# Row maxima of both score blocks of an attention unit in one VectorE instruction, with both exponentials behind it, in a two-layer diffusion backbone

## The chip, the cores and the metric

The kernel runs on one core of a Trainium2 chip, as one program. The metric is the time of that core on the device in microseconds (us); lower is better. TensorE (PE) multiplies matrices, VectorE (DVE) and ScalarE (ACT) work elementwise, GpSimd (POOL) gathers, and each engine runs its own instructions in the order in which they are written. Engines wait for each other through semaphores alone: an instruction behind a wait that is not yet met stays where it is, and so does all that is queued behind it on the same engine.

## What is computed

Two layers, each of them a normalisation, a combined projection, three token mixers side by side (RWKV-7 time mixing, differential attention, a gated linear recurrence), an output projection, and then a retrieval of experts with product keys. The change lies in the differential attention. For each head and each block of 128 queries there are two score blocks, `c = 0` and `c = 1`, of half the head's dimension each:

```python
s = jnp.einsum('bhqcd,bhkcd->bhcqk', qi, k).astype(jnp.float32) * scale
p = jax.nn.softmax(s, axis=-1)
p = p[:, :, 0] - lam * p[:, :, 1]
return jnp.einsum('bhqk,bhkd->bhqd', p.astype(v.dtype), v)
```

The softmax takes the maximum of each row off before the exponential, so each block needs its row maxima first. The 512 latent tokens attend to 768 keys (512 of their own and 256 cached), the 128 prompt tokens to 128.

## The kernel before

One stage per layer, `mix_stage`, runs the RWKV-7 scan and the attention together. Nothing is planned at run time: the order is written out by hand as a list of **slots**, and every engine walks the same list. The scan is the backbone of it. It has 5 steps of 14 hops (`HOPS`: pairs, lower, square1 to square5, inverse, rhs0, sa0, state0, rhs1, sa1, state1), so 70 slots. In each slot PE does the products of the hop (`hop`), DVE and sometimes ACT take them out of PSUM (`take`), and PE starts the next hop when DVE has raised `byv` and, after the square hops, ACT has raised `bya`.

The attention is laid into those slots as 40 **units** per layer (`UNITS`: one head, one block of 128 tokens; units 0 to 31 are latent with 768 keys, units 32 to 39 are prompt with 128). Slots are counted in threes. In the first slot of three, the even unit 2p gets its scores, row maxima and exponentials; in the third, the odd unit 2p+1. In between stands the second slot, where earlier units get their products with the values. For one unit the chain is:

- `scores` on PE (L1245, or L1248 to L1252): both blocks into PSUM banks 4 to 7. The banks are not doubled, so it first waits for `e_done`, until both exponentials of the unit before are through.
- `row_max` on DVE (L1444): one reduction for each block, each raising `m_ready`.
- `exps` on ACT (L1323): one exponential for each block with the negated maximum as bias and the row sum as accumulated output (a separate read of the accumulator follows each); each raises `e_done`.
- `weights` on DVE (L1449, L1450): reciprocals of the sums, after both exponentials. Then `scale_second` on ACT (L1328), `combine` on DVE (L1458), `turn` on PE (L1265, transposes through PSUM bank 3), `take_turned` on ACT (L1335), `values` on PE (L1284) and `out` on DVE (L1464), which also frees bank 3 (`o_taken`) for the next `turn`.

The order on each engine within a slot matters here. PE: the hop, `turn` of the first half of an older unit, `scores` of the new unit, `turn` of the second half. DVE: the hop's `take`, then in first slots `combine` and `weights` of the unit before, then `row_max` of the new unit; in second slots `weights` of the even unit, `combine`, `out`. ACT: the hop's `take` (copies L1339, L1346, L1349, L1354), `take_turned`, in first slots `scale_second` of the odd unit before, and at the end `exps` of the new unit. So the exponentials stand directly ahead of ACT's copy for the next hop. PE also multiplies some filler (L1133) in hops where it would idle.

Of the kernel before, what the change touches and what calls it, by code (L numbers as in the profile page):

```python
# [31 lines left out]
ALU = mybir.AluOpType  # L32
ACT = mybir.ActivationFunctionType
AX = mybir.AxisListType

P = 128
# [960 lines left out]
KH = 3 * P  # L997


def key_halves(u):  # L1000

    return 2 if UNITS[u][1] < TILES - 1 else 1


def half_count(u, half):

    return sum(key_halves(i) for i in range(u)) + half + 1


def is_unit(u):  # L1010
    return 0 <= u < len(UNITS)


def both_halves(u):
    return range(key_halves(u)) if is_unit(u) else ()
# [5 lines left out]
def mix_stage(g, l, keep):  # L1021
# [17 lines left out]
    s_ready, m_ready, e_done, r_ready, scaled = (  # L1039
        g.sem(x) for x in ("scores_ready", "row_max_ready", "exps_ready", "weights_ready", "second_scaled"))  # L1040
    comb, t_ready = g.sem("probs_combined"), g.sem("probs_transposed")
    pt_ready, o_ready, o_taken = g.sem("probsT_ready"), g.sem("attn_out_ready"), g.sem("attn_out_taken")
    A, B, C, W, S = 0, 1, 2, 3, 4
    OUT = CA * P
    with ExitStack() as st, nc.Block() as block:
# [13 lines left out]
        p = g.sb(st, "p", [P, 2, 2, 2, KH])  # L1059
        pd = g.sb(st, "pd", [P, 2, 2 * KH])  # L1060
        pt = g.sb(st, "pt", [P, 2, 2 * KH])
        mx = g.sb(st, "mx", [P, 2, 2])
# [13 lines left out]
        def scores_of(u, c):  # L1076

            b = S + 2 * c
            return g.ps[:, b:b + 2, 0:KH] if key_halves(u) == 2 else g.ps[:, b:b + 1, 0:P]

        def probs_of(u, c):
            return p[:, u % 2, c, :, :] if key_halves(u) == 2 else p[:, u % 2, c, 0:1, 0:P]

        def flat_probs(u, c):
            whole = p[:, u % 2, c, :, :].rearrange("p k n -> p (k n)")
            return whole if key_halves(u) == 2 else whole[:, 0:P]

        def half_keys(u, k):

            return slice(k * KH, (k + 1) * KH) if key_halves(u) == 2 else slice(0, P)  # L1090

        @block.sync
        def _(sync):
            sync.dma_start(mask[:, :, :], d["consts"][:, CI["maskF"][0]:CI["maskF"][0] + 4 * CH]).then_inc(loaded, 16)
            sync.dma_start(low[:, :, :], d["consts"][:, CI["lowF"][0]:CI["lowF"][0] + 3 * CH]).then_inc(loaded, 16)
            sync.wait_ge(zeroed, 1)
            for h in range(2):
                rows = slice(h * HD, (h + 1) * HD)
                sync.dma_start(sz[rows, :, :, h * HD:(h + 1) * HD], d["state_rwkv"][l, h]).then_inc(state_in, 16)

            sync.wait_ge(final, 1)
            for h in range(2):
                rows = slice(h * HD, (h + 1) * HD)
                sync.dma_start(d["new_rwkv"][l, h], sz[rows, :, :, h * HD:(h + 1) * HD]).then_inc(stored, 16)
# [212 lines left out]
        @block.scalar  # L1317
        def _(act):
            def exps(u, c):
                act.wait_ge(m_ready, 2 * u + c + 1)  # L1320
                if u >= 2:
                    act.wait_ge(comb, u - 1)
                nc.scalar.activation(probs_of(u, c), scores_of(u, c), ACT.Exp,  # L1323
                                     bias=mx[:, u % 2, c:c + 1], accum_out=sm[:, u % 2, c:c + 1]).then_inc(e_done, 1)

            def scale_second(u):
                act.wait_ge(r_ready, u + 1)
                nc.scalar.activation(flat_probs(u, 1), flat_probs(u, 1), ACT.Copy, scale=sm[:, u % 2, 3:4]).then_inc(scaled, 1)  # L1328

            def take_turned(u, k):  # L1330
                keys = half_keys(u, k)
                act.wait_ge(t_ready, half_count(u, k))
                if u >= 2:
                    act.wait_ge(o_ready, u // 2)
                nc.scalar.activation(pt[:, u % 2, keys], g.ps[:, W, 0:keys.stop - keys.start], ACT.Copy).then_inc(pt_ready, 1)  # L1335

            def take_keys(n):
                act.wait_ge(bt_ready, n)
                nc.scalar.activation(bt[:, (n - 1) % 2, :, :].rearrange("p i n -> p (i n)"), g.ps[:, (B, C)[n % 2], :], ACT.Copy).then_inc(bt_taken, 1)  # L1339

            def take(slot, step, name):
                if name.startswith("square"):
                    act.wait_ge(ready, slot + 1)
                    n = int(name[6:])
                    if n == 1:
                        nc.scalar.activation(pw, by_unit(A), ACT.Copy).then_inc(bya, 1)  # L1346
                        take_keys(2 * step + 2)
                    else:
                        nc.scalar.activation(pwt[:, (n + 1) % 2, :, :], by_unit(C), ACT.Copy).then_inc(bya, 1)  # L1349
                elif name == "lower":  # L1350
                    take_keys(2 * step + 1)
                elif name == "inverse":
                    act.wait_ge(tok_ready, step + 1)
                    nc.scalar.activation(tv[:, :, :], g.ps[:, B, :].rearrange("p (i n) -> p i n", i=2), ACT.Copy).then_inc(tok_taken, 1)  # L1354

            for slot, (step, name) in enumerate(SLOTS):
                take(slot, step, name)
                pair, third = divmod(slot, 3)
                if third == 1:
                    if is_unit(2 * pair):  # L1360
                        scale_second(2 * pair)
                else:
                    u, fresh = (2 * pair - 3, 2 * pair) if third == 0 else (2 * pair - 2, 2 * pair + 1)
                    for k in both_halves(u):
                        take_turned(u, k)
                    if third == 0 and is_unit(fresh - 1):
                        scale_second(fresh - 1)
                    if is_unit(fresh):
                        for c in range(2):
                            exps(fresh, c)  # L1370

        @block.vector
        def _(ve):
# [65 lines left out]
                                    o.did(last)  # L1439
                return last  # L1440

            def row_max(u, c):
                ve.wait_ge(s_ready, u + 1)
                ve.tensor_reduce(mx[:, u % 2, c:c + 1], scores_of(u, c), AX.XY, ALU.max, negate=True).then_inc(m_ready, 1)  # L1444

            def weights(u):

                ve.wait_ge(e_done, 2 * u + 2)
                o.then(ve.reciprocal(sm[:, u % 2, 2:4], sm[:, u % 2, 0:2]))  # L1449
                ve.tensor_scalar(sm[:, u % 2, 3:4], sm[:, u % 2, 3:4], g.lam[:, 1:2], None, ALU.mult).then_inc(r_ready, 1)  # L1450

            def combine(u):

                ve.wait_ge(scaled, u + 1)
                if u >= 2:
                    ve.wait_ge(t_ready, half_count(u - 2, key_halves(u - 2) - 1))
                n = flat_probs(u, 0)
                ve.scalar_tensor_tensor(pd[:, u % 2, 0:n.shape[-1]], n, sm[:, u % 2, 2:3], flat_probs(u, 1),  # L1458
                                        ALU.mult, ALU.add).then_inc(comb, 1)

            def out(u):
                h, t = UNITS[u]
                ve.wait_ge(o_ready, u // 2 + 1)
                ve.tensor_copy(g.outT[:, CA + h // 2, t * P:(t + 1) * P], g.ps[:, W, KH:KH + P]).then_inc(o_taken, 1)  # L1464
# [5 lines left out]
            for slot, (step, name) in enumerate(SLOTS):  # L1470
                ve.wait_ge(ready, slot + 1)
                nx += name in XSUMS
                take(step, name, nx).then_inc(xsum if name in XWITH else byv, 1)
                if step == TILES - 1 and name == "state1":
                    ve.wait_ge(byv, slot + 1)
                    ve.sem_inc(final, 1)
                pair, third = divmod(slot, 3)
                if third == 0:
                    if is_unit(2 * pair - 2):
                        combine(2 * pair - 2)  # L1480
                    if is_unit(2 * pair - 1):
                        weights(2 * pair - 1)
                elif third == 1:
                    if is_unit(2 * pair):
                        weights(2 * pair)
                    if is_unit(2 * pair - 1):
                        combine(2 * pair - 1)
                    if is_unit(2 * pair - 3):
                        out(2 * pair - 3)
                if third != 1 and is_unit(2 * pair + third // 2):  # L1490
                    for c in range(2):
                        row_max(2 * pair + third // 2, c)
    return stored


# [1494 lines left out]
```

## Time and profile before

| | |
|---|---|
| median of 3 runs | 4174.37 us (4172.11 to 4175.89) |
| profiled execution, first to last instruction (its span) | 4170.2 us |
| what the median has over the span | 4.2 us |
| PE busy | 3967.5 us, 95% |
| DVE busy | 3319.0 us, 80% |
| ACT busy | 1514.5 us, 36% |

The profile gives no other time of the profiled execution than its span; 4.2 us is what the median of the runs lies above it. Busy time says how long an engine had an instruction in work, not that it set the pace. Times in rows are microseconds from the start of the span, unless marked ns. `x2` at the end of a row of the timeline says that two instructions of the same kind stand in it one after the other. An idle time in brackets names the instruction that ended it.

### The profile page before, as it was taken

To read this page: it belongs to the slowest core of one execution; us is meant where nothing else is said; L and a number is where in the kernel's file an instruction comes from. 1 tells how busy PE (TensorE), PEld (TensorE's weight loads), DVE (VectorE), ACT (ScalarE), POOL (GpSimd) and SP (SyncE) were. 2 spreads that over 40 slices of the span, in tenths; PEclk is the share of its full clock that TensorE was granted. 3 is DMA by queue.
4 is the path that set the end of the run, shared out by engine and by line. 5 is a ranking of instruction groups with operands and counts; after the bars stand their busy time and mean duration, and the time that the engine had idled before them with its cause. 6 is when DMAs were issued, how large, how long until landed. Compare 5 with 4: busy or idle time off the path is not lost. (4 is left out here: it accounts for less than half of the span.)

```text
span 4170.2 us, 69350 instructions
## 1 busy us (share of the span) xinstructions
PE 3967.5 (95%) x25830; PEld 3126.4 (75%) x25830; DVE 3319.0 (80%) x6259; ACT 1514.5 (36%) x2457; POOL 1426.5 (34%) x1046
## 2 busy tenths in 40 slices
PE   7999988999999999999989999889999999999997
PEld 5977767655567888888879677775555788888886
DVE  3556753799998999999955676538999899999997
ACT  3435643211164333333353355321112633333333
POOL 0010000265414656666500000004644066566662
PEclk8999999999999999999999899899999999999998
DMA  6230013799999999999822300157998999999996
GB/s 254 71 137 6 2 38 117 246 369 333 342 302 356 393 400 398 406 404 404 346 92 60 127 2 2 53 179 294 350 342 320 302 391 407 389 408 403 404 406 252
DMA packets 410253, 1095.17 MB, mean 263 GB/s; under 512 B 38288, under 2 KB 181008, under 8 KB 403344
## 3 DMA queue, kind: packets, MB, share of 16 engines
q1 hardware_dynamic: 262544, 554.96, 36.9%
q0 software_dynamic: 147456, 536.94, 33.2%
q8 instruction: 147, 2.41, 0.2%
q14 instruction: 106, 0.87, 0.1%
HBM read 1013.90 MB, written 77.86 MB: 262 GB/s over the span
## 5 line engine op out<-in xcount | busy, mean ns | idle before, releaser
L1822 POOL DMA_INDIRECT ring<-peer_u_rows,rows x512 | 670.5, 1310 | 1785.0 <-DVEq L2176 1077.6
L1822 POOL DMA_INDIRECT ring<-peer_v,rows x512 | 731.4, 1428 | 431.3 <-DVE acc L2663 359.2
L1779 PE MATMUL ps<-h,u 128*128 128x384 f32 x2112 | 700.3, 489 | 3.4 <-PEq L1895 2.5
L2663 DVE SCALAR_TENSOR_TENSOR acc<-ring,act,acc 128x1024 f32<-128x1024 f32 x508 | 643.1, 1279 | 1.7
L1826 DVE SCALAR_TENSOR_TENSOR ring<-ring,acc 128x1024 f32<-128x1024 f32 x512 | 613.7, 1219 | 34.4 <-PEq L2292 22.7
L200 PE MATMUL ps<-vhi,wlo 128*128 128x512 f32 x1536 | 603.9, 393 | 22.0 <-DVE wlo L2642 21.0
L201 PE MATMUL ps<-vlo,whi 128*128 128x512 f32 x1536 | 600.7, 391 | 0.0
L202 PE MATMUL ps<-vhi,whi 128*128 128x512 f32 x1536 | 600.5, 391 | 0.0
L1779 PEld LDWEIGHTS ps<-h,u 128*128 128x128 f32 x2112 | 396.1, 191 | 261.9 <-issue 6.8
L2627 DVE TENSOR_TENSOR vlo<-v,vhi 128x1024 fp32r<-128x1024 f32 x256 | 312.4, 1220 | 77.9 <-ACT vhi L2570 71.4
L200 PEld LDWEIGHTS ps<-vhi,wlo 128*128 128x128 f32 x1536 | 289.6, 189 | 91.2 <-issue 32.4
L200 PE MATMUL ps<-xhi,ulo 128*128 128x384 f32 x992 | 332.6, 335 | 2.6 <-DVE ulo L2623 2.6
L202 PEld LDWEIGHTS ps<-vhi,whi 128*128 128x128 f32 x1536 | 289.4, 188 | 60.7
L201 PEld LDWEIGHTS ps<-vlo,whi 128*128 128x128 f32 x1536 | 289.6, 189 | 58.7
L202 PE MATMUL ps<-xhi,uhi 128*128 128x384 f32 x992 | 332.7, 335 | 0.0
L201 PE MATMUL ps<-xlo,uhi 128*128 128x384 f32 x992 | 332.2, 335 | 0.0
L2570 ACT ACTIVATE vhi<-v 128x1024 fp32r<-128x1024 f32 x256 | 269.1, 1053 | 117.4 <-DMA v<-peer_v 105.1
L1950 PE MATMUL ps<-h,query_raw 128*128 128x128 f32 (+1 forms) x1024 | 295.3, 443 | 8.5 <-ACT h L419 8.4
L1790 ACT ACTIVATE hh<-ps 128x384 f32<-128x384 f32 x256 | 123.1, 481 | 440.6 <-PE ps L1779 396.3
L2575 ACT ACTIVATE whi<-u 128x384 fp32r<-128x384 f32 x128 | 63.7, 525 | 599.8 <-DVE u L2637 599.8
L1950 PEld LDWEIGHTS ps<-h,query_raw 128*128 128x128 f32 x1024 | 162.7, 197 | 126.1 <-issue 115.0
L200 PE MATMUL ps<-hhi,proj_lo 128*128 128x320 f32 x672 | 211.7, 315 | 24.3 <-DVE hlo L439 24.3
(356 smaller groups left out, 7092.2 us busy)
## 6 DMA issues: line engine op xcount, KB each, us to landing
u<-peer_u SPq DMA_DIRECT2D x256, 512.0 KB
v<-peer_v SPq DMA_DIRECT2D x256, 512.0 KB
gates<-stage SPq DMA_DIRECT2D x24, 1984.0 KB, 9.7
sel<-gates SPq DMA_DIRECT2D x62, 768.0 KB
query_raw<-peer_wq SPq DMA_DIRECT2D x64, 512.0 KB
hidden<-hh SPq DMA_DIRECT2D x128, 192.0 KB
u<-hidden SPq DMA_DIRECT2D x128, 192.0 KB
mod_ring<-mod_late SPq DMA_DIRECT2D x20, 1024.0 KB, 8.5
```

Source lines behind the costliest of these rows:

```text
L200: pe.matmul(out, lhs[1], rhs[0], start=start, stop=False)
L201: pe.matmul(out, lhs[0], rhs[1], start=False, stop=False)
L202: return pe.matmul(out, lhs[0], rhs[0], start=False, stop=stop)
L1779: mm = pe.matmul(self.g.ps[:, bank, 0:ND], self.u[:, slot, kc, :], self.x[:, kc, 0:ND], start=(kc == 0), stop=(kc == KC - 1))
L1790: return self.g.nc.scalar.activation(self.hh[:, slot, :], self.g.ps[:, slot, 0:ND], ACT.Gelu)
L1822: return pool.indirect_dma_start(to, None, table, rows)
L1826: return ve.scalar_tensor_tensor(row, row, 1.0, self.acc[:, x, :], ALU.mult, ALU.mult, accum_out=self.act[x][:, slot:slot + 1])
L1950: return pe.matmul(g.ps[:, SUMS + i % 2, 0:width(i)], raw[:, i % Q_RING, kc, :], h[:, kc, tokens_of(i)], start=(kc == 0), stop=(kc == KC - 1))
L2570: nc.scalar.activation(v2[0][:, j, :], v[:, j % 2, :], ACT.Copy).then_inc(v_hi, 1)
L2575: nc.scalar.activation(w2[0][:, j, :], h, ACT.Copy).then_inc(w_hi, 1)
L2627: ve.tensor_tensor(v2[1][:, j, :], v[:, j % 2, :], v2[0][:, j, :].bitcast(F32), ALU.subtract).then_inc(v_lo, 1)
L2663: ve.scalar_tensor_tensor(acc, r, w, acc, ALU.mult, ALU.add).then_inc(used, 1)
```

## The change

The two reductions of a unit become one, over both blocks, which writes both maxima and raises `m_ready` once. Both exponentials wait for that one.

```diff
@@ mix_stage, ACT
             def exps(u, c):
-                act.wait_ge(m_ready, 2 * u + c + 1)
+                act.wait_ge(m_ready, u + 1)
@@ mix_stage, DVE
-            def row_max(u, c):
+            def row_max(u):
                 ve.wait_ge(s_ready, u + 1)
-                ve.tensor_reduce(mx[:, u % 2, c:c + 1], scores_of(u, c), AX.XY, ALU.max, negate=True).then_inc(m_ready, 1)
+                both = g.ps[:, S:S + 4, :].rearrange("p (c k) n -> p c k n", c=2)
+                scores = both[:, :, :, 0:KH] if key_halves(u) == 2 else both[:, :, 0:1, 0:P]
+                ve.tensor_reduce(mx[:, u % 2, :], scores, AX.XY, ALU.max, negate=True).then_inc(m_ready, 1)
@@ the slot loop, DVE
                 if third != 1 and is_unit(2 * pair + third // 2):
-                    for c in range(2):
-                        row_max(2 * pair + third // 2, c)
+                    row_max(2 * pair + third // 2)
```

## Rows read from the trace of the kernel before

**Rows 1.** The page: the span.

```profile
span 4170.2 us, 69350 instructions
```

**Rows 2.** Busy time of each engine in the two mixing stretches, one per layer.

```profile
core 0: us, PE busy (x) PEld busy (x) DVE busy (x) ACT busy (x) POOL busy (x), PEclk, DMA share, GB/s
320.00:590.00 270.00, 250.26 (x3981) 197.90 (x3974) 179.17 (x369) 147.48 (x308) 0.00 (x0) 0.96 0.01 3
2370.00:2640.00 270.00, 250.49 (x3942) 198.12 (x3942) 178.07 (x367) 147.47 (x308) 0.00 (x0) 0.95 0.01 2
```

**Rows 3.** Waits in 320 to 590: us in total, times, longest us.

```profile
PEld ps L1248 <- ACT p L1323: 7.0, 8, 1.2
```

**Rows 4.** Groups by line and shape on DVE: count, busy us, mean ns, idle before.

```profile
L1444 DVE TENSOR_REDUCE mx<-ps 128x1 f32<-128x768 f32 x128 | 116.4, 951 | 49.4 <-PE ps L1252 49.4
L1444 DVE TENSOR_REDUCE mx<-ps 128x1 f32<-128x128 f32 x32 | 7.7, 283 | 4.4 <-PE ps L1245 4.4
L2168 DVE TENSOR_REDUCE sm<-res 128x8 f32<-128x128 f32 x10 | 2.8, 280 | 0.0
```

**Rows 5.** Timeline around unit 5: start us, us, engine, line, idle time in brackets.

```profile
360.64 1.82 DVE L1444 TENSOR_REDUCE mx<-ps 128x1 f32<-128x768 f32 x2 [1.89 <-PE ps L1252]
...
361.63 0.90 ACT L1323 ACTIVATE p<-ps,mx 128x768 f32<-128x768 f32 x1
...
363.31 0.20 ACT L1323 ACTIVATION_READ_ACCUMULATOR p<-ps,mx 128x1 f32 x1
...
363.56 0.30 PEld L1248 LDWEIGHTS ps<-proj 32*128 32x128 f32 x4 [1.16 <-ACT p L1323]
```

**Rows 6.** Timeline behind units 3 and 11: last sum, next scores.

```profile
351.08 0.20 ACT L1323 ACTIVATION_READ_ACCUMULATOR p<-ps,mx 128x1 f32 x1
...
351.69 0.30 PEld L1248 LDWEIGHTS ps<-proj 32*128 32x128 f32 x4 [0.17 <-issue]
...
404.88 0.20 ACT L1323 ACTIVATION_READ_ACCUMULATOR p<-ps,mx 128x1 f32 x1
...
405.88 0.30 PEld L1248 LDWEIGHTS ps<-proj 32*128 32x128 f32 x4 [0.17 <-issue]
```

**Rows 7.** Timeline: PE's hop behind unit 2.

```profile
343.46 1.04 PEld L1165 LDWEIGHTS ps<-pwt,px 64*64 64x64 f32 x32 [1.73 <-DVE px L1407]
```

**Rows 8.** Timeline around unit 14, up to PE's wait for the combined weights.

```profile
421.23 1.82 DVE L1444 TENSOR_REDUCE mx<-ps 128x1 f32<-128x768 f32 x2 [0.87 <-PE ps L1252]
...
422.91 0.89 ACT L1323 ACTIVATE p<-ps,mx 128x768 f32<-128x768 f32 x1
...
424.80 0.17 DVE L1449 RECIPROCAL sm<-sm 128x2 f32<-128x2 f32 x1 [1.43 <-ACT p L1323]
...
426.46 0.31 PEld L1265 LDWEIGHTS ps<-keep,pd 128*128 128x128 f32 x3 [1.28 <-DVE pd L1458]
```

**Rows 9.** Timeline around unit 16, the same chain.

```profile
434.92 1.81 DVE L1444 TENSOR_REDUCE mx<-ps 128x1 f32<-128x768 f32 x2
...
436.02 0.89 ACT L1323 ACTIVATE p<-ps,mx 128x768 f32<-128x768 f32 x1
...
439.57 0.31 PEld L1265 LDWEIGHTS ps<-keep,pd 128*128 128x128 f32 x3 [1.29 <-DVE pd L1458]
```

**Rows 10.** Timeline behind unit 22: ACT's copy for the hop, and the hop.

```profile
479.18 0.60 ACT L1349 ACTIVATE pwt<-ps 128x512 f32<-128x512 f32 x1
...
480.02 1.01 PEld L1188 LDWEIGHTS ps<-px,pwt 64*64 64x64 f32 x32 [0.17 <-issue]
```

**Rows 11.** Timeline: maxima of units 24 and 25, first and second layer.

```profile
488.67 1.82 DVE L1444 TENSOR_REDUCE mx<-ps 128x1 f32<-128x768 f32 x2 [1.13 <-PE ps L1252]
497.35 1.82 DVE L1444 TENSOR_REDUCE mx<-ps 128x1 f32<-128x768 f32 x2 [0.59 <-PE ps L1252]
...
2536.91 1.82 DVE L1444 TENSOR_REDUCE mx<-ps 128x1 f32<-128x768 f32 x2 [1.13 <-PE ps L1252]
2547.17 1.82 DVE L1444 TENSOR_REDUCE mx<-ps 128x1 f32<-128x768 f32 x2 [0.59 <-PE ps L1252]
```

**Rows 12.** Clock in a stretch between the last two (columns as in Rows 2).

```profile
2537.80:2541.00 3.20, 3.20 (x26) 2.43 (x24) 1.74 (x6) 2.72 (x7) 0.00 (x0) 0.50 0.00 0
```

**Rows 13.** Timeline: PE's longest wait in the first stretch.

```profile
566.46 0.86 PEld L1143 LDWEIGHTS ps<-ar,proj 64*64 64x64 f32 x32 [2.75 <-DVE outT L1437]
```

## The prediction

> **What bounds the kernel now.** I read the page first: PE is busy for 95% of a span of 4170.2 us [rows 1], so at first sight nothing on DVE matters. But the changed instructions lie in two stretches only, one per layer, so I read the busy times there: in each 270 us PE is busy for 250, DVE for 179, ACT for 147 [rows 2]. No engine is full. PE has some 20 us of idle time per stretch, and the work goes round in a circle: PE makes products, DVE and ACT take them, PE waits for the taking. The question is thus which waits of PE end on the chain that the change lengthens. The waits in the stretch answer it: PE's load of query weights for the next unit's scores waits 8 times for an exponential, 7.0 us in all [rows 3], and the second layer's stretch shows the same wait with the same count and sum.
>
> The timeline of one of them, unit 5, shows the chain [rows 5]. The two reductions start at 360.64 and end together 1.82 us later. The first exponential starts at 361.63, 0.99 us after the first reduction started: that is its 0.95 us [rows 4] and 0.04 of signal. Both exponentials and the reads of their sums end at 363.51, and 0.05 us later PE starts the next scores. PE had then idled for 1.16 us. The second reduction lies wholly beside the first exponential. So the chain is: first maximum, two exponentials, PE. That is what the change touches.
>
> **The merged instruction.** It replaces two of 951 ns (768 elements) by one over 1536, in 32 units per layer, and two of 283 ns (128 elements) by one over 256 in 8 units. From the two shapes an element costs (951 - 283) / 640 = 1.04 ns [rows 4]. So 951 + 768 x 1.04 = 1.75 us, and 0.42 us for the short ones. A second result in each partition should cost nothing: the reduction with eight results takes 280 ns where one result takes 283 [rows 4]. Bounds: 1.60 us if the fixed part shrinks to nothing, and 1.90 us, twice the single one. I take 1.75, since two in a row take 1.82 with two fixed parts [rows 5]. DVE is freed by 0.07 us per unit. The first exponential, though, no longer starts at R + 0.99 (R: start of the reduction) but at R + 1.75 + 0.04 = R + 1.79. Everything behind it comes 0.80 us later, unless ACT was held until later anyway. That is the price, and the places where it counts follow.
>
> **Odd units (third slots).** ACT's only other work ahead of the exponentials is the copy of turned weights, which ends at about R + 0.96, so the full 0.80 us is lost. What PE feels is 0.80 less its slack beyond the 0.05 us of signal. I went through all units of the first layer for the distance from the last sum to PE's next scores. Units 1, 5, 7, 9, 13, 23, 25 and 27 have 0.05 us (unit 5 in [rows 5]), so these cost 8 x 0.80 = 6.40 us. Units 3, 19 and 31 have 0.41 (unit 3: 351.28 to 351.69 [rows 6]), 0.43 each, 1.29 us. Units 11, 17, 21 and 29 have 0.80 (unit 11: 405.08 to 405.88 [rows 6]), 0.03 to 0.05 each, 0.18 us. Unit 15 has more and costs nothing. The prompt units cost almost nothing, since their reductions lie under ACT's other work; 0.08 us at unit 35. Behind unit 31 a short unit follows, and ACT's next two copies then hold PE's second turn: 0.28 us more.
>
> **Even units (first slots).** Here ACT first rescales the odd unit before. In units 6, 8, 14, 20, 24, 26 and 28 that holds the exponential until R + 1.68 (unit 14: 421.23 to 422.91 [rows 8]), so only 0.11 us is lost. In units 0, 2, 4, 10, 12, 16, 18, 22 and 30 DVE itself was late, R is late, and 0.38 to 0.81 us are lost at the exponential. PE does not wait for these exponentials directly, but for two chains behind them:
>
> - Sums, weights, combination, `out`, then PE's turn. At unit 14 DVE idles 1.43 us for the sum and PE 1.28 us for DVE [rows 8]: 0.11 us. At unit 16 the exponential starts at R + 1.10 [rows 9], and 1.79 - 1.10 = 0.69 us arrive at PE's wait at 439.57. At unit 18, 0.40, and at unit 4, 0.12 on top of what unit 3 has already shifted.
> - ACT's copy for the next hop, queued behind the exponentials. At unit 22 it ends at 479.78 and PE starts at 480.02 [rows 10]; a loss of 0.66 less 0.24 of slack, with 0.05 to 0.10 of signal, is 0.47 us beyond unit 21. At unit 30, 0.45; at unit 12, 0.09; at unit 28, 0.09; at unit 0, 0.36.
>
> Unit 2 adds nothing: PE's hop at 343.46 [rows 7] waits for this copy and for DVE, and both were going to come 0.80 us later, DVE because PE is shifted behind unit 1, ACT because of unit 2. The two delays lie side by side. Unit 10 is covered in the same way by unit 9.
>
> The even terms come to 0.11 + 0.69 + 0.40 + 0.12 + 0.47 + 0.45 + 0.09 + 0.09 + 0.36 = 2.78 us. With the odd terms, 6.40 + 1.29 + 0.18 + 0.08 + 0.28 = 8.23 us, it is 11.0 us per layer and **22.0 us** for both.
>
> Does a later wait swallow it? PE's delay arises before it does the new scores, so all that DVE and ACT do from those is delayed too, and the next waits shift with it. The one exception is a wait for something DVE began before PE was delayed; I found that at unit 17 alone, worth 0.03 us. What DVE gains, 0.07 us, ends in DVE's own waits for PE (49.4 us idle ahead of the maxima alone [rows 4]).
>
> **The clock.** PE's waits grow from 1.16 to nearly 2 us at five odd units per layer, and unit 16's likewise. In the second layer such a wait, of the same size as unit 5's, was followed by a stretch at a granted clock of 0.50, the 1.2 GHz level [rows 12]. Between the maxima of units 24 and 25 passed 10.26 us there, and 8.68 in the first layer, which kept its clock [rows 11]: 1.58 us lost. Of some 20 waits of 1.0 to 1.8 us in both layers one had that; of the two of 2.75 us (the first in [rows 13]) both had. Waits of 2 us lie in between, a dozen of them. I take three more such stretches, 4.7 us; bounds none and ten, 0 to 16 us. The Trainium skill ("TensorE: Matmul & The Clock Gate", What's actually happening) says that the throttled state is the default and activity releases it; the two rows agree as far as they go.
>
> **The sum**, against the profiled execution: 4170.2 + 22.0 + 4.7 = 4196.9 of span, and with the 4.2 us that the median has over the span, 4201.1 us, +0.64%. The bounds of the merged instruction, 1.60 and 1.90 us, move the 17 or so terms of a layer by 0.15 each: 5 us less or more. The likeliest case's own range is 4190 to 4212.
>
> **The rivals.**
> - *Delays that lie side by side* (0.14). As at unit 2, more of the terms may overlap than I saw: PE waits for both an engine that it delayed itself and one that was late by itself. If it is half of all terms, 11 us remain, 4185; if two thirds, 7 us, 4181.5, which counts as no change. For it: the even units where DVE was late. Against: the largest terms are waits with nothing else due.
> - *The clock falls often* (0.09): ten stretches or more, 22 + 16 and up, 4212 to 4225. For it: rows 11 and 12; against: one in twenty now.
> - *DVE is relieved and that decides* (0.03), the faster side. In a third of the slots DVE's maxima run straight into the next take. Should PE wait for DVE behind them nearly everywhere, the saving of 0.07 us counts for each of 80 units, 5 us, 4169. It decides only where ACT is held beyond R + 1.79 for other reasons, which no latent unit shows. The Trainium skill ("VectorE: DVE Perf Modes", Rules for kernel authors) speaks for this change: it says to minimise the number of operations, since each one drains the pipe. By that rule the pair costs twice 0.95 us and the merge saves 0.15 us a unit, 12 us in all, 4162. The trace shows 1.82 for the pair, so less than half of that.
> - *The reduction does not run as one* or runs at another rate (0.02): at 1.90 us and beyond, 4206 and up. The same page (The perf-mode tier table) gives this operation one rate only; rows 4 agree with 1.04 ns per element. A rate that would bring 1536 elements under 0.95 us, from where the exponentials would come no later, is thus not to be expected.
>
> **How the numbers follow.** The main case has 0.72. What a measurement of this kernel can tell from no change is about 0.2%, 8 us. Slower by more than that: the main case, the clock, the slow reduction, and about half of the side-by-side case, together 0.90. Within 8 us: the rest of the side-by-side case and half of the relieved one, 0.08. Faster: 0.02. The range goes from 4184, which takes in the half-overlapping case, to 4215, which takes in ten clock stretches' lower part.
>
> **What would show it.** The reduction at 1.75 us, 64 long and 16 short ones in place of 160; the first exponential of odd units at R + 1.79; PE's wait for the exponential in 11 or more places per layer instead of 9 and of about 2 us where it was 1.16; the stretch from the first to the last maximum 11 us longer per layer; nothing changed between the stretches. I am wrong if the reduction takes far from 1.75 us, if PE's waits grow but the stretch does not, or if the stretches with a granted clock of 0.50 multiply.

## The result, and the profile after

The changed kernel takes 4221.3 us in the median of 4 runs (4215.8 to 4236.1), the kernel before 4175.1 us (4172.1 to 4177.8): a ratio of 1.0119, with an interval of 1.0100 to 1.0138. A second series on another occasion gave 1.0123 (1.0100 to 1.0146). It is slower by some 50 us. The forecast was slower too, but by 27 us, with a range that ended at 4215. The time lies outside of it.

The profiled execution of the changed kernel is the longest of its four, 4236.1 us with a span of 4234.2, so it is 64 us above the span of rows 1. The page first:

```profile
span 4234.2 us, 69270 instructions
PE 4013.8 (95%) x25830; PEld 3157.9 (75%) x25830; DVE 3318.0 (78%) x6179; ACT 1514.6 (36%) x2457; POOL 1425.0 (34%) x1046
```

80 instructions fewer, all of them on DVE (6179 for 6259). PE does the same 25830 products, yet is busy for 46 us more. The products are as many, so they got slower, and the clock is the first thing to ask. The groups by line and shape on DVE answer to rows 4:

```profile
L1446 DVE TENSOR_REDUCE mx<-ps 128x2 f32<-128x1536 f32 x64 | 112.3, 1755 | 62.9 <-PE ps L1252 62.8
L1446 DVE TENSOR_REDUCE mx<-ps 128x2 f32<-128x256 f32 x16 | 6.7, 420 | 4.4 <-PE ps L1245 4.1
```

1755 and 420 ns: the merged instruction runs as it was estimated, 1.75 and 0.42 us. The timeline around unit 5 answers to rows 5 (start, duration, engine, line; idle time in brackets):

```profile
366.76 1.76 DVE L1446 TENSOR_REDUCE mx<-ps 128x2 f32<-128x1536 f32 x1 [1.89 <-PE ps L1252]
...
368.56 0.90 ACT L1323 ACTIVATE p<-ps,mx 128x768 f32<-128x768 f32 x1 [0.83 <-DVE mx L1446]
...
370.23 0.20 ACT L1323 ACTIVATION_READ_ACCUMULATOR p<-ps,mx 128x1 f32 x1
...
370.48 0.30 PEld L1248 LDWEIGHTS ps<-proj 32*128 32x128 f32 x4 [1.96 <-ACT p L1323]
```

The first exponential starts 1.80 us after the reduction where it was 0.99, and PE's wait is 1.96 us instead of 1.16. ACT is now idle for 0.83 us ahead of the exponential. Unit 22 answers to rows 10: ahead of PE's next hop, where PE had been idle for 0.17 us, it is now idle for 0.61 us. The profile names no releaser here ("issue"), but ACT's copy had ended 0.07 us before the hop started, where it had been 0.24 us.

```profile
502.25 1.75 DVE L1446 TENSOR_REDUCE mx<-ps 128x2 f32<-128x1536 f32 x1
...
505.80 0.59 ACT L1349 ACTIVATE pwt<-ps 128x512 f32<-128x512 f32 x1
...
506.46 1.04 PEld L1188 LDWEIGHTS ps<-px,pwt 64*64 64x64 f32 x32 [0.61 <-issue]
```

The waits of the first mixing stretch answer to rows 3 (total, times, longest): 13 where there were 8, and 2.0 us at most.

```profile
PEld ps L1248 <- ACT p L1323: 15.2, 13, 2.0
```

Now the two stretches from the first to the last maximum of a layer, as busy times of each engine with the granted clock in the column behind POOL. First the kernel before:

```profile
324.60:583.50 258.90, 239.85 (x3829) 189.84 (x3831) 174.19 (x358) 145.03 (x300) 0.00 (x0) 0.96 0.01 2
2373.00:2634.80 261.80, 242.90 (x3831) 192.20 (x3833) 174.32 (x358) 145.01 (x300) 0.00 (x0) 0.95 0.01 2
```

and the changed one:

```profile
329.00:619.20 290.20, 263.99 (x3825) 207.73 (x3827) 173.50 (x319) 145.29 (x300) 0.00 (x0) 0.88 0.01 2
2411.40:2697.50 286.10, 259.86 (x3823) 204.56 (x3825) 173.29 (x318) 145.57 (x300) 0.00 (x0) 0.89 0.01 2
```

Of the 64 us, 55.6 lie here (576.3 for 520.7). The other 8.4 us are not shown to come from the change: a second profile of the changed kernel, further below, is 55.5 us above rows 1, and 55.3 of them lie in the same two stretches. DVE and ACT are as busy as before; PE is busy for 41 us more. The clock has only two levels here, 1.00 and 0.50, so a mean of 0.88 over 290.2 us is 2 x 0.12 x 290.2 = 70 us at the lower one. The printed mean is rounded to 0.01, which over such a stretch can hide some 2.6 us. So the times at the lower clock from here on are summed from windows laid around each fall: 43 us for both stretches before and 133 us after, a rise of 90 us. These are the five falls of the kernel before:

```profile
324.60:332.70 8.10, 7.02 (x118) 6.17 (x119) 4.41 (x10) 3.69 (x7) 0.00 (x0) 0.50 0.01 2
568.20:578.40 10.20, 8.85 (x128) 7.48 (x128) 5.54 (x17) 3.25 (x13) 0.00 (x0) 0.50 0.01 2
2373.00:2380.70 7.70, 6.62 (x116) 5.78 (x116) 4.12 (x9) 3.40 (x6) 0.00 (x0) 0.50 0.00 0
2537.70:2541.10 3.40, 3.40 (x30) 2.63 (x26) 1.94 (x6) 2.92 (x7) 0.00 (x0) 0.50 0.00 0
2616.20:2629.80 13.60, 12.31 (x170) 10.39 (x170) 6.76 (x22) 3.93 (x14) 0.00 (x0) 0.50 0.01 1
```

Two of them are the tail of a lower clock that the stretch begins with, two stand at the wait of 2.75 us near its end, and only 3.4 us lie anywhere between. The changed kernel has sixteen. Within its first stretch it looks like this:

```profile
358.00:371.60 13.60, 11.46 (x162) 8.50 (x160) 8.78 (x15) 8.35 (x17) 0.00 (x0) 1.00 0.01 2
371.80:381.80 10.00, 10.00 (x89) 8.23 (x87) 4.80 (x9) 4.01 (x7) 0.00 (x0) 0.50 0.01 2
460.50:477.40 16.90, 16.90 (x147) 13.03 (x145) 9.16 (x18) 5.94 (x12) 0.00 (x0) 0.50 0.00 1
```

The clock falls some 1.2 us after unit 5's wait of 1.96 us has ended, and stays down for 10 us. After unit 16's wait it stays down for 17 us: the maxima of units 17 and 18 are 9.85 us apart where they were 7.28 (441.67 to 448.95). Beside the lower clock that this stretch begins with, it falls seven times in it, each time within 1.5 us of the end of a wait of 1.49 to 1.98 us: at units 5, 7, 9, 16, 23, 25 and 27. DVE's rows of the changed kernel:

```profile
372.34 1.76 DVE L1446 TENSOR_REDUCE mx<-ps 128x2 f32<-128x1536 f32 x1 [1.46 <-PE ps L1252]
385.02 1.76 DVE L1446 TENSOR_REDUCE mx<-ps 128x2 f32<-128x1536 f32 x1 [2.03 <-PE ps L1252]
...
462.32 1.76 DVE L1446 TENSOR_REDUCE mx<-ps 128x2 f32<-128x1536 f32 x1 [2.73 <-PE ps L1252]
472.17 1.75 DVE L1446 TENSOR_REDUCE mx<-ps 128x2 f32<-128x1536 f32 x1
```

The first two are units 6 and 7: 12.68 us, and 8.86 before.

### The profile page after: what moved, and what is told of

Read it like the earlier page. It is cut to its first block and busy times, and to the rows that moved or that the text cites. A ratio compares the mean times of both kernels' runs of the same rounds, so it can differ in the third digit from the quotient of the medians.

```text
span 4234.2 us, 69270 instructions
## 1 busy us (share of the span) xinstructions
PE 4013.8 (95%) x25830; PEld 3157.9 (75%) x25830; DVE 3318.0 (78%) x6179; ACT 1514.6 (36%) x2457; POOL 1425.0 (34%) x1046
```

## The experiments

Theory A has two parts. The first exponential starts later, which costs latency, 22 us by the sum. The longer waits of PE bring the lower clock, and that costs the rest. Against it stand three others: that the merged instruction itself does harm (B), that the latency was undercounted and the clock is a by-product (B2), and that all units lose alike. Ratios are to the kernel before on the same chip.

### Both exponentials wait, nothing merged

```diff
-                act.wait_ge(m_ready, 2 * u + c + 1)
+                act.wait_ge(m_ready, 2 * u + 2)
```

> The kernel before with its two reductions, but both exponentials wait for both maxima; nothing is merged. Theory A (the cost is the first exponential's start, plus the clock stretches that the longer waits of PE bring): the first exponential of odd units starts at R + 1.86 instead of R + 1.79, so all of the changed kernel's loss and some 2 us more, 1.010 to 1.015 of before, with the stretches at a granted clock of 0.50 as many as in the changed kernel. Theory B (the merged reduction itself costs, by its shape or by what it does to PSUM): at most a third of the loss, under 1.004.

Measured: 1.0131 (1.0111 to 1.0151), 4228.3 us, so the whole loss is there with two reductions. The timeline around unit 5 shows 1.86 us from the maxima to the exponential and PE's wait of 2.02 us:

```profile
359.15 1.82 DVE L1444 TENSOR_REDUCE mx<-ps 128x1 f32<-128x768 f32 x2 [1.88 <-PE ps L1252]
361.01 0.90 ACT L1323 ACTIVATE p<-ps,mx 128x768 f32<-128x768 f32 x1 [0.90 <-DVE mx L1444]
...
362.94 0.30 PEld L1248 LDWEIGHTS ps<-proj 32*128 32x128 f32 x4 [2.02 <-ACT p L1323]
```

The stretches from first to last maximum are 575.6 us long, 122 us of it at the lower clock. Theory B falls: it is the waiting that costs. The 2 us more that merging should save are less than the runs can tell.

### The merged instruction over half of the keys

```diff
-                scores = both[:, :, :, 0:KH] if key_halves(u) == 2 else both[:, :, 0:1, 0:P]
+                scores = both[:, :, :, 0:KH // 2] if key_halves(u) == 2 else both[:, :, 0:1, 0:P]
```

> The changed kernel with the merged reduction over the first 192 of each 384 score columns, 768 elements in place of 1536 (the maxima of the other half of the keys are left out). One instruction for both blocks as in the changed kernel, with the duration of one of the old ones, 0.95 us. Theory A: the first exponential is back at R + 0.99, PE's waits at 1.16 us, and the loss is gone: 0.998 to 1.001, with as many stretches at a granted clock of 0.50 as before. If merging itself cost something (one signal for both, the shape), a loss would stay.

Measured: 0.9989 (0.9974 to 1.0004), no difference that can be told. The merged reduction and its waiting:

```profile
L1446 DVE TENSOR_REDUCE mx<-ps 128x2 f32<-128x768 f32 x64 | 61.1, 955 | 50.2 <-PE ps L1252 50.2
PEld ps L1248 <- ACT p L1323: 7.0, 8, 1.2
```

With 0.955 us for one instruction in place of 1.755, PE's waits are those of rows 3 to the digit, and the added time at the lower clock is gone: 0.97 in both stretches, 35 us of their 516.2 at the lower level. One instruction and one signal for both blocks cost nothing. What costs is that the first exponential waits 0.80 us longer. It also shows that relieving DVE buys next to nothing: against the kernel before, DVE is busy for 52 us less (3266.9 for 3319.0), and the time is the same.

### Merged in odd units alone, in even units alone

Two kernels of the same edit: `merged(u)` is `u % 2 == 1` in one and `u % 2 == 0` in the other. `row_max` branches on it in the same way.

```diff
+def merged(u):
+    return u % 2 == 1
+def maxima_before(u):
+    return sum(1 if merged(i) else 2 for i in range(u))
...
-                act.wait_ge(m_ready, 2 * u + c + 1)
+                act.wait_ge(m_ready, maxima_before(u + 1) if merged(u) else maxima_before(u) + c + 1)
```

> Merged in odd units alone (third slots), two reductions in even units. By the sum of the prediction the odd units cost 8.2 us per layer, 16.5 us in all, without the clock. Theory A adds the clock, since the waits of 2 us lie behind odd units: 30 to 42 us, 1.007 to 1.010. If the loss comes evenly from all units, half of it: 1.006.

> Merged in even units alone (first slots), two reductions in odd units. PE's waits for the exponentials of odd units stay at 1.16 us. By the sum of the prediction some 4 us per layer, 8 us in all (2.8 us, and what units 2, 4 and 10 no longer hide behind the odd unit before them), and Theory A expects hardly more clock stretches than before: 1.001 to 1.004. If the loss comes evenly from all units: 1.006.

Measured: odd alone 1.0081 (1.0063 to 1.0099), even alone 1.0034 (1.0020 to 1.0047). The loss does not come evenly from all units: odd alone lose 36 us in the medians and even alone 13.5, and the two add up to the whole. PE's waits for the exponentials, odd alone first and then even alone:

```profile
PEld ps L1256 <- ACT p L1331: 15.5, 14, 2.0
```

```profile
PEld ps L1256 <- ACT p L1331: 7.0, 8, 1.2
```

The waits for the exponentials grow with the odd units alone. The lower clock does not. These are the stretches, in the same order:

```profile
328.00:604.20 276.20, 251.78 (x3824) 198.26 (x3826) 174.28 (x339) 144.40 (x300) 0.00 (x0) 0.92 0.01 2
2398.80:2673.40 274.60, 248.96 (x3825) 196.02 (x3827) 173.97 (x339) 144.22 (x300) 0.00 (x0) 0.93 0.01 2
```

```profile
329.70:596.80 267.10, 245.55 (x3831) 193.99 (x3833) 173.56 (x339) 146.24 (x300) 0.00 (x0) 0.94 0.01 2
2386.40:2658.40 272.00, 251.78 (x3831) 198.91 (x3833) 173.44 (x338) 146.24 (x300) 0.00 (x0) 0.92 0.01 2
```

Odd alone has 81 us at the lower level and even alone 74, where the kernel before has 43. I had expected hardly more of it for the even units, and that was wrong, although this profile is of the longest of its ten executions (4202.0 us for a median of 4188.4). PE does not wait for the even units' exponentials, but it waits for the combination behind them: at unit 16 that wait is 1.98 us where it was 1.29, and the clock falls 1.3 us behind it, for 14 us.

### The clock alone

The kernel before without its own filler products. They feed nothing.

```diff
-                if name in ("rhs0", "rhs1", "sa0", "sa1"):
-                    fill(C)
-                elif name == "state0":
-                    fill(A)
```

> The kernel before without its own filler products in rhs, sa and state0 hops (they feed nothing). No latency of the chain grows; PE only idles where it multiplied filler. It measures the clock alone. Theory A: more stretches at a granted clock of 0.50 between the first and the last maximum, and the time grows by some 0.37 us for each us of them, which is what the profiles so far show: with 60 to 100 us more of them, 20 to 40 us slower, 1.005 to 1.010. If the clock is no cause of its own, the time stays or falls by the filler's few tenths per hop.

Measured: 1.0045 (1.0026 to 1.0065), 16 us slower with 50 products fewer (25 per layer, two instructions each in the profile) and no signal later. Its stretches:

```profile
327.20:598.50 271.30, 247.68 (x3789) 196.51 (x3791) 174.55 (x358) 144.92 (x300) 0.00 (x0) 0.89 0.01 2
2382.30:2653.50 271.20, 247.45 (x3791) 197.00 (x3793) 174.63 (x359) 144.88 (x300) 0.00 (x0) 0.89 0.01 2
```

They are 21.8 us longer than before with some 119 us at the lower clock, 76 more. PE's longer idling alone does it. The price per us at the lower clock is 0.29 here, less than the 0.37 I had taken, and whatever the filler itself had cost is already taken off it. The time came out just below the expectation.

### More filler in both kernels

```diff
+                    free = {"rhs0": (C, 0), "rhs1": (C, 0), "sa0": (C, 0), "sa1": (C, 0), "inverse": (A, 0)}.get(name)
+                    if third == 2 and free and name != "inverse":
+                        fill(*free)
+                        fill(*free)
                     if is_unit(u):
                         turn(u, 0)
+                    if third == 0 and free and is_unit(fresh):
+                        for _ in range(2 if name == "inverse" else 3):
+                            fill(*free)
```

> The changed kernel with more filler products on PE (the same 128x256 product that it has already), put where PE would wait: two ahead of the turn and three ahead of the wait for the exponentials in rhs and sa slots, two in inverse slots. They change no latency of the chain. Theory A: most stretches at a granted clock of 0.50 between the first and the last maximum go, and with them their part of the loss; what is left is the latency, 22 us by the sum, 1.004 to 1.008. Theory B2 (the latency was undercounted, the clock is only a by-product): the loss stays at 1.010 or more.

> The control of the filled kernel: the kernel before with the same additional filler products, and its own two reductions. It gives the filler's own price, and the difference of the two filled kernels is the change's price with the clock held. Theory A: that difference is the latency, 22 us. The profiles so far: the filled changed kernel has 14.9 us per layer over the kernel before in undisturbed distances from unit to unit where the sum had 11.0, so the filler should cost some 4 us per layer here: 0 to 8 us slower than before, 0.999 to 1.002. Theory B2 (latency undercounted): the difference of the filled kernels is over 30 us.

Measured: the changed kernel with filler 1.0048 (1.0036 to 1.0060), 4196.5 us; the kernel before with the same filler 0.9992 (0.9978 to 1.0006), 4171.1 us. The stretches of the filled changed kernel:

```profile
328.30:602.70 274.40, 254.87 (x3887) 201.38 (x3889) 172.81 (x318) 145.82 (x300) 0.00 (x0) 0.96 0.01 2
2385.30:2661.50 276.20, 256.85 (x3889) 203.84 (x3891) 172.85 (x319) 146.20 (x300) 0.00 (x0) 0.95 0.01 2
```

The clock is back where it was in the kernel before (0.96 and 0.95, 46 us at the lower level), with the latency chain unchanged and more work on PE, and over half of the loss is gone. B2 falls. Between the two filled kernels lie 25.4 us in the medians, against 22.0 us of the sum; they ran on two chips, and by their ratios it is 23 us, with an interval of some 16 to 31. In the profiles the two differ by 19.6 us in the stretches, and there the clock was not quite held: the filled kernel before has 36 us at the lower level, 10 fewer. So this confirms the latency roughly and not finely.

The filler has a price of its own. The stretches of the filled kernel before are 531.0 us long, 10.3 more than without it, and yet its median is no longer. The profile does not explain that: it is of the longest of eleven executions, 4187.7 us, and shows nothing won outside of the stretches either. This stays open.

### PE's scores by block

To win something: PE does block 0's scores after the first exponential of the unit before, and block 1's after the second.

```diff
-                    pe.wait_ge(e_done, 2 * u)
+                    pe.wait_ge(e_done, 2 * u - (t != TILES - 1))
...
                     for c, r in enumerate(rows):
+                        if c == 1 and u >= 1:
+                            pe.wait_ge(e_done, 2 * u)
                         pe.matmul(g.ps[:, S + 2 * c, 0:KH], q[c], keys(r, 0, KH), start=True, stop=True)
-                    for c, r in enumerate(rows):
                         pe.matmul(g.ps[:, S + 2 * c + 1, 0:NS - KH], q[c], keys(r, KH, NS), start=True, stop=True)
-                    for c, r in enumerate(rows):
```

> The kernel before, with PE's scores put in order by block: all three products of block 0 after the first exponential of the unit before, those of block 1 after the second. If PE's wait is for the second exponential alone, it gets about 0.7 us back at each of 8 odd units per layer, 11 us in all, 0.997. Against it: the two blocks lie in different rows of the array and may run partly beside each other when they alternate, as they do now (four loads of 384 columns in 0.92 us); one after the other they may take 0.3 to 0.9 us longer in each of 64 units, 20 to 60 us slower.

Measured: 1.0113 (1.0087 to 1.0140). The wait went from 7.0 us to 1.3 us in all, as meant, but the group of the 384-column products (busy, mean ns) grew. The kernel before, then this one, 330 to 600:

```profile
L1248 PE MATMUL ps<-proj 32*128 32x384 f32 x124 | 28.4, 533 | 5.1 <-ACT p L1323 4.9
```

```profile
L1250 PE MATMUL ps<-proj 32*128 32x384 f32 x124 | 53.5, 546 | 0.2
```

So the second of the two expectations came true, 20 to 60 us slower. The mean of one product is nearly the same (546 ns for 533) and the time that they cover is nearly doubled, 25 us more in this layer. The two blocks lie in different rows of the array and, alternated, run beside each other. The 42 us of loss are not this alone: the two stretches have 81 us at the lower clock here, 38 more than before, and how much of the loss is the clock's was not separated.

### The changed kernel again, and both gains together

> The changed kernel once more, beside the kernel before on the same chip, for the size of its loss and for a second profile of its clock. Theory A: 1.009 to 1.014, with 100 us or more between the maxima at a granted clock of 0.50 and the two stretches longer by 22 us plus 0.37 us for each us of it beyond the 43 us of the kernel before.

Measured: 1.0123 (1.0100 to 1.0146), 4225.2 us. The stretches are 576.0 us long, 129 us of it at the lower clock: nearly as in the first profile. The expectation, 520.7 + 22 + 0.37 x (129 - 43) = 574.5, is 1.5 us short.

> The changed kernel with the reduction over half of the keys (the maxima of the other half are left out) and the additional filler products. If the two gains add up, 0.997 to 0.999 of before; if ACT's copy, which ends at R + 0.96, and PE's own work set the pace, no difference that can be measured: 0.999 to 1.000.

Measured: 1.0005 (0.9991 to 1.0018), 4174.1 us. The gains do not add up: the clock is 0.98 in both stretches, only 16 us at the lower level, but they are 524.9 us long, 4 us more than before. No kernel tried here beats the kernel before by more than the runs can tell.

## Why the prediction was wrong

**What bounds the stretch: right.** PE in a circle with DVE and ACT, waiting for the second exponential of the odd unit before. The kernel in which both exponentials wait without a merge has the whole loss.

**The merged instruction: right.** 1755 ns for 1.75 us, 420 for 0.42, and no price for the second result.

**The latency terms: right, within what can be seen.** Distances from one unit's maxima to the next in which neither kernel had the lower clock can be compared directly. In the second layer there are 24 of 39. They sum to 6.4 us more than before; the sum's terms for the same distances give 6.6 to 7.0, by how much of unit 9's 0.80 us is put behind unit 9 (0.42 was measured there) and how much behind unit 10. Behind units 7, 13 and 23 it is 0.80 as predicted, behind 19 it is 0.43, behind 22 it is 0.52 for 0.52, behind 3 and 4 together 0.55 for 0.55, behind 14 it is 0.13 for 0.11, behind 31 and 32 together 0.65 for 0.71, behind 35 it is 0.09 for 0.08. Units 1 and 2 lay side by side as foreseen, and so did 9 and 10 as far as they can be seen. Two terms were off: behind unit 12 it is 0.18 for 0.09, and behind units 29 and 30 together only 0.19 for 0.50, since in the kernel before unit 30's reduction was late on DVE by 0.35 us that the changed kernel does not have. The other 15 distances were disturbed by the clock in one kernel or the other, though PE's waits there grew by the 0.80 us (units 5, 23 and 25: 1.16 or 1.18 to 1.96 or 1.98). The changed kernel with more filler shows five of them without the lower clock. Against the kernel before, the distances behind units 5, 23 and 25 are longer by 0.79 to 0.80 us, behind unit 16 by 0.68 for 0.69, and behind unit 18 by 0.40 for 0.40. The terms of units 0 and 28 and the rest of unit 9's are not confirmed.

**The clock: the step that failed.** I took "three more such stretches, 4.7 us", at 1.58 us each, with ten and 16 us as the bound. In the profile 55.6 us were added in the two stretches. Less 22.0 of latency, 33.6 are left, seven times the 4.7 us and twice the bound; by the medians it is 24 to 33 us, five to seven times. There were eleven more falls and not three (sixteen for five), and the lower clock lasted longer: 8.3 us a fall in the mean, 10 after unit 5 and 17 after unit 16, where the one case that I priced, rows 11 and 12, lasted 3.4. The price of a microsecond was not too small: 33.6 us for 90 more at the lower clock is 0.37 each, and rows 11 give 1.58 for 3.4, which is 0.46.

The number came from counting: one wait in twenty of 1.0 to 1.8 us, two in two of 2.75 us, so I put a dozen waits of 2 us at a quarter. A single case and two others do not fix a chance in between, and I chose near the low end. The shorter waits, 1.49 us at unit 9 and 1.80 at unit 27, were followed by falls as well. The means of rows 2, 0.96 and 0.95, would not have helped: 40 of the 43 us behind them lie at the start of the stretches and at the wait of 2.75 us, and between them the clock was full but for 3.4 us. What was there to be read is the filler. I read it as something that fills idle time and never asked what it was for; without it the kernel before loses 16 us.

**What the loss is made of.** With the latency at 22 us, the medians' 46 to 55 us leave 24 to 33 us for the clock. That the clock is a cause of its own is shown from two sides: less filler brings a loss with no signal later, and more filler takes over half of the loss away with no signal of the chain earlier. The split to the microsecond is an estimate.

**The rivals.** "The clock falls often" is what happened, and it had only 0.09. Its 4212 to 4225 held the first median and ends at the second, but with a price of 1.58 us a stretch it would have needed 15 to 20 more of them; there were eleven more, and longer ones. "Delays that lie side by side" fell with the 24 distances. "DVE is relieved" fell with the reduction over half of the keys. The Trainium skill's rule to minimise the number of VectorE operations ("VectorE: DVE Perf Modes", Rules for kernel authors) holds for DVE's own time, 0.07 us a unit here, and says nothing of who waits for the first of two results.

The prediction cited the Trainium skill on the clock ("TensorE: Matmul & The Clock Gate", What's actually happening): the lower level is the default and activity releases it. The kernel before agrees, with a mean clock in its stretches of 0.89 without its filler, 0.96 and 0.95 as it was, and 0.97 with more filler.

## What to carry to other kernels

Merging two reductions into one saves a few hundredths of a microsecond on the engine that does them and delays the first result by the length of the second. Where the consumer was starting on the first, that delay goes straight into the circle of engines, so look for who waits for the first result before counting instructions. And when a change lengthens waits of PE in a stretch that carries filler products, ask how often the clock will fall and how long it will stay down, and do not price it by one instance: here it cost more than the latency itself. Look also at where in the stretch the lower clock lies, since a mean over the whole of it does not say.

## What the runs showed of the hardware

- In the kernel before, a wait of PE of 1.1 to 1.2 us was followed by a lower clock once. With waits of 1.96 us at the same places the two stretches had 129 to 133 us at the 1.2 GHz level, in both profiles. The length of a wait does not decide alone: with even units merged, a wait of 1.16 us was followed by the lower level in the first layer (2.6 us later, for 7 us) and the same wait in the second layer was not.
- Each microsecond at the lower level cost 0.29 us (filler removed) to 0.39 us (second profile of the changed kernel, 33.3 us for 86) in the mean. Single places differ more: 2.57 us for 9.85 between units 17 and 18, which is 0.26, and 1.58 for 3.4 in rows 11, which is 0.46.
- Where the clock falls repeats: the distance between the maxima of units 17 and 18 was 9.85 us, wholly at the lower level, in both layers of both profiles of the changed kernel.
- Products over 32 rows of the array, in different rows, ran beside each other when they alternated and not when they stood in order by block: 124 of them cover 28.4 us in the one and 53.5 us in the other. The Trainium skill says of products over few rows in distinct row groups that they run at the same time ("TensorE: Matmul & The Clock Gate", Why this matters for your kernels). The rows agree for the alternated order; that the order decides is shown by these two kernels alone.
